# Seam of merge, routing and experts in a one-core encoder block: a wait moved, a tail reordered, small work moved between engines, and the last norm put into the experts stage

## The chip, the cores and the metric

The kernel runs on one core of one Trainium2 chip. The metric is the device time of one execution in microseconds (us), the median of several runs. A profiled execution has its own time, and inside it the span from its first instruction to its last.

## What is computed

One layer of a streaming encoder over 2048 tokens of 1024 features: two attention branches, a gated merge with an output projection, a mixture of experts (top group of 4, then the top 2 of its 8 experts), a last RMSNorm. Only the part from the merge's end on matters here:

```python
x = x + mixed @ w_out[l]
h2 = rmsnorm(x, norm_ffn[l])
x = x + hierarchical_moe(h2, ...)      # in it:
    g_logits = hf @ w_rg + b_rg                 # 4 groups
    e_logits = hf @ w_re + b_re                 # 32 experts
    g_sel = argmax(g_logits); top_v, top_i = top_k(e_logits of the group, 2)
    gate_w = p_group * softmax(top_v)
    # each expert's rows, in order of token, in tiles; for each tile
    a = silu(xb @ w_eg[e]) * (xb @ w_eu[e]);  y = a @ w_ed[e]
    out[row_tok] += y * row_w
return rmsnorm(x, norm_final)
```

All matrix products are float32 in three products of parts: each operand is split into a high part (rounded to fp32r) and the remaining low part (names `_hi`, `_lo`). ScalarE writes the high parts, VectorE and GpSimd the low ones.

## The kernel before

The program is a chain of stages (`project`, `attend`, `merge`, `route`, `experts`, `finish`). In a stage each engine has its own instruction list, in the order in which the code is written, and the engines meet only through semaphores. Between stages all engines meet: the block ends with a drain and a barrier (L60), then `Stage.__exit__` clears the stage's semaphores on GpSimd and runs another barrier (L63, L64). Three stages close together after the experts: `ex`, `weights` and `routes`; after `finish` one closes (`fn`).

**merge** goes over 8 blocks of 256 tokens, each with two tiles t of 128. TensorE runs block 0 apart and blocks 1 to 7 as one loop (`over_block`). At a block's end it multiplies the mixed rows with `w_out` (8 steps k of 6 products for each t, L1639). VectorE adds x (L1565), takes part in the RMS statistics and writes the normed row h (L1569); ScalarE squares, takes the root and stores x2 and h2. The router's logits of a tile need h turned by TensorE (`turn_h`, L1593), copied to SBUF as hT by ScalarE (`copy_h`, L1437), multiplied with the router's weights (`route_h`, L1600) and biased on VectorE (`logits`, L1532). For blocks 0 to 6 this happens inside the next block; for the last one it stands at the very end, tile 0 and then tile 1.

**route** works on all 2048 tokens at once, mostly as one chain on VectorE in which each operation waits for the one before (`then`). Constants are set first (13 memsets on VectorE, L1818 to L1821). Group and experts are picked with one-hot tensors laid out [token tile t, expert e]. Two products count rows: `upper` x `both` gives the rank within a tile, `ones` x `both` the sum of each tile. VectorE adds up the 16 tiles' sums one after another (`base`, L1869), adds the rank (L1870), and from slot numbers builds one-hot tensors: `tile_is` (L1892), `row_hot` (L1895), `tile_hot` parts 0 and 1 (L1898, L1900). Part 2, the low part of the weights, is on GpSimd (L1773). TensorE gathers them in 32 products (L1798), which are read out at L1907 to L1912. SyncE meanwhile loads expert 0's weights.

**experts** goes over 32 experts, each with at least one tile of 128 rows, with the weights of the next expert split while the current one is computed. TensorE's `step` for tile n is: gate product, turn of the previous tile's a, up product, turn of the next tile's x (`turn_x`), and the down product of the previous tile; in the very first step that down product has a zero `a` behind it. For expert 0 the wait for its down weights' low parts (`d_lo_pool`, `d_lo_dve`) stands ahead of the whole step. GpSimd gathers rows of h2 and adds result rows to x2 by indirect DMA (L2012); its last act is to wait until these are in DRAM.

**finish** loads x2 again, 16 tiles of 128 rows of 4 KB, through 8 input buffers by SyncE's queue, and g_row (`norm_final` on all partitions); ScalarE squares, takes roots, VectorE does the rest (`mean_square`, `inverse_rms`, L2319), GpSimd's queue stores the 16 tiles from 4 buffers (L2289).

## Time and profile before

| what | value |
|---|---|
| median of 3 runs | 2535.26 us (2533.03 to 2535.77) |
| the profiled execution | 2534.02 us |
| its span | 2532.3 us |
| TensorE busy in the span | 2304.2 us, 91% |
| VectorE, ScalarE, GpSimd busy | 51%, 40%, 34% |
| merge's last product ends to the first expert product | about 1570 to 1657 us of the span |
| last row added by the experts to the end | about 2476 to 2532 us |

The profile lists for each engine what ran when, what it did between (idle, with the inferred releaser), the granted TensorE clock (1.00 is 2.4 GHz, 0.50 is 1.2 GHz), and the DMA engines' share. TensorE is nearly always busy inside a stage; the idle stretches lie at the seams.

### The profile page before, as it was taken

Reading aid. Unit: us, or ns where it says so; the run is one execution under the profiler, and the core shown is the slowest. Engines: PE = TensorE matmul, PEld = TensorE weight load, DVE = VectorE, ACT = ScalarE, POOL = GpSimd, SP = SyncE. Lnnn points to the kernel's source line nnn. Section 1 sums busy time; section 2 is a strip of 40 time slices with the busy share of each in tenths; the row PEclk is TensorE's granted clock in tenths of the full one; section 3 lists DMA queues with packets and bytes.
Section 4 is the critical chain, followed back from the end, with each engine's and each line's share of the span. In section 5 each row is a group of like instructions: output and inputs, shape, how many; then the busy total and the mean of one; then the engine's idle time right before and its main releaser. Section 6 shows DMA issues by size and latency. Waiting matters only on the chain. (4 is left out here: it accounts for less than half of the span.)

```text
span 2532.3 us, 36785 instructions
## 1 busy us (share of the span) xinstructions
PE 2304.2 (91%) x12238; PEld 1976.1 (78%) x12239; DVE 1303.3 (51%) x1953; ACT 1023.1 (40%) x1778; POOL 854.8 (34%) x796
## 2 busy tenths in 40 slices
PE   7999999999996889986999998289999999999990
PEld 5888888888885788885999998268888888888870
DVE  5112223111002777775433333767857768788874
ACT  6111112111113777773222211146646556667653
POOL 5354665520000111112223221134444535455451
PEclk9999999999998999998999999589999999999995
DMA  5357757531115676636544442479978979899977
GB/s 179 106 148 263 251 173 240 177 115 61 73 58 200 172 229 170 196 83 205 179 140 141 141 141 91 144 240 307 321 227 272 327 226 323 281 370 346 317 254 282
DMA packets 234881, 517.34 MB, mean 204 GB/s; under 512 B 24368, under 2 KB 90032, under 8 KB 233648
## 3 DMA queue, kind: packets, MB, share of 16 engines
q1 hardware_dynamic: 159104, 342.28, 39.1%
q0 software_dynamic: 32352, 95.18, 15.0%
q10 hardware_dynamic: 43344, 78.86, 8.7%
q8 instruction: 44, 0.72, 0.1%
q14 instruction: 37, 0.30, 0.0%
HBM read 384.56 MB, written 131.66 MB: 204 GB/s over the span
## 5 line engine op out<-in xcount | busy, mean ns | idle before, releaser
L440 DVE TENSOR_TENSOR pj_w_lo<-pj_w_raw,pj_w_hi 128x1024 fp32r<-128x1024 f32 x38 | 48.0, 1263 | 520.0 <-ACT pj_w_hi L314 520.0
L314 ACT ACTIVATE pj_w_hi<-pj_w_raw 128x1024 fp32r<-128x1024 f32 x38 | 40.2, 1059 | 529.9 <-PE pj_bank L538 477.7
L2024 POOL TENSOR_TENSOR ex_wd_lo<-weights_raw_d,ex_wd_hi 128x1024 fp32r<-128x1024 f32 x64 | 199.4, 3138 | 124.1 <-ACT ex_wd_hi L2052 124.1
L538 PE MATMUL pj_bank<-pj_hT_hi,pj_w_lo 128*128 128x512 f32 x896 | 239.5, 389 | 0.0
L538 PE MATMUL pj_bank<-pj_hT_hi,pj_w_hi 128*128 128x512 f32 x896 | 239.5, 389 | 0.0
L538 PE MATMUL pj_bank<-pj_hT_lo,pj_w_hi 128*128 128x512 f32 x896 | 239.5, 389 | 0.0
L538 PEld LDWEIGHTS pj_bank<-pj_hT_lo,pj_w_hi 128*128 128x128 f32 x896 | 168.2, 188 | 34.9
L538 PEld LDWEIGHTS pj_bank<-pj_hT_hi,pj_w_hi 128*128 128x128 f32 x896 | 168.2, 188 | 34.9
L538 PEld LDWEIGHTS pj_bank<-pj_hT_hi,pj_w_lo 128*128 128x128 f32 x896 | 168.2, 188 | 34.8
L2106 DVE TENSOR_TENSOR ex_wd_lo<-weights_raw_d,ex_wd_hi 128x1024 fp32r<-128x1024 f32 x64 | 164.4, 2607 | 5.0 <-ACT ex_wd_hi L2052 4.9
L1615 PE MATMUL mg_y_ps<-mg_aT_hi,mg_w_hi 128*128 128x256 f32 x512 | 148.9, 291 | 9.8 <-DVE mg_gated L1526 6.6
L2172 PE MATMUL ex_g_ps<-ex_wg_hi,ex_xT_hi 128*128 128x512 f32 x360 | 141.0, 392 | 13.9 <-DVE ex_wd_lo L2106 13.9
L2100 DVE TENSOR_TENSOR ex_wu_lo<-weights_raw_u,ex_wu_hi 128x1024 fp32r<-128x1024 f32 x128 | 152.3, 1249 | 2.1
L2172 PE MATMUL ex_y_ps<-ex_wd_hi,ex_aT_hi 128*128 128x512 f32 x368 | 148.6, 404 | 1.9 <-DVE ex_aT_lo L2112 1.9
L2100 DVE TENSOR_TENSOR ex_wg_lo<-weights_raw_g,ex_wg_hi 128x1024 fp32r<-128x1024 f32 x128 | 147.8, 1214 | 3.6 <-ACT ex_wg_hi L2052 3.6
L854 POOL DMA_DIRECT2D scratch_attT<-at_o_both x60 | 49.7, 866 | 288.2 <-DMA scratch_attT<-at_o_both 288.2
L1390 POOL TENSOR_TENSOR mg_gated<-mg_gated 128x256 f32<-128x256 f32 x64 | 53.7, 840 | 274.0 <-DVE mg_gated L1526 273.5
L1616 PE MATMUL mg_y_ps<-mg_aT_lo,mg_w_hi 128*128 128x256 f32 x512 | 145.8, 285 | 0.0
L1617 PE MATMUL mg_y_ps<-mg_aT_hi,mg_w_lo 128*128 128x256 f32 x512 | 145.8, 285 | 0.0
L2172 PE MATMUL ex_u_ps<-ex_wu_hi,ex_xT_hi 128*128 128x512 f32 x360 | 144.9, 402 | 0.0
L2172 PE MATMUL ex_y_ps<-ex_wd_lo,ex_aT_hi 128*128 128x512 f32 x368 | 144.7, 393 | 0.0
L2172 PE MATMUL ex_y_ps<-ex_wd_hi,ex_aT_lo 128*128 128x512 f32 x368 | 143.7, 391 | 0.0
(289 smaller groups left out, 5920.1 us busy)
## 6 DMA issues: line engine op xcount, KB each, us to landing
weights_raw_g<-in_w_exp_gate_dram SPq DMA_DIRECT2D x128, 512.0 KB
weights_raw_u<-in_w_exp_up_dram SPq DMA_DIRECT2D x128, 512.0 KB
weights_raw_d<-in_w_exp_down_dram SPq DMA_DIRECT2D x128, 512.0 KB
pj_w_raw<-in_w_feat_dram SPq DMA_DIRECT2D x38, 512.0 KB, 4.8
scratch_gates<-pj_f_hi ACTq DMA_DIRECT2D x32, 512.0 KB, 5.0
mg_g_in<-scratch_gates SPq DMA_DIRECT2D x128, 128.0 KB, 3.1
pj_x_in<-in_x_dram SPq DMA_DIRECT2D x16, 512.0 KB, 3.6
scratch_qk<-pj_f_hi ACTq DMA_DIRECT2D x16, 512.0 KB, 5.1
```

The costliest lines, as they stand in the source:

```text
L314: act.activation(w_hi[n % 2][:], w_raw[n % 2][:], ACT.Copy).then_inc(whi_done, 1)
L440: dve.tensor_tensor(w_lo[n % 2][:], w_raw[n % 2][:], w_hi[n % 2][:], ALU.subtract).then_inc(wlo_done, 1)
L538: last = pe.matmul(eight[4 * p + b][:], w[p][:, k * P:(k + 1) * P], h[:, k, b * NB:(b + 1) * NB], start=(k == 0 and n == 0), stop=(k == KD ...
L854: pool.dma_start(attT[A_COLS + hd * DH:A_COLS + (hd + 1) * DH, at:at + WIDE], o_both[pair % 4][DH:, :], accum_op=ALU.add).then_inc(lo_out[ ...
L1390: pool.tensor_tensor(mixed[o % 2], gated[o % 2][:, :MB], gated[o % 2][:, MB:], ALU.add).then_inc(mixed_done, 1)
L1615: pe.matmul(y, w_hi[:, k, cols], aT_hi[:, k, :], start=(k % 4 == 0), stop=False)
L1616: pe.matmul(y, w_hi[:, k, cols], aT_lo[:, k, :], start=False, stop=False)
L1617: last = pe.matmul(y, w_lo[:, k, cols], aT_hi[:, k, :], start=False, stop=(k % 4 == 3))
L2024: pool.tensor_tensor(wd_lo[p][:, j, :], raw.buffer[2][j][:], wd_hi[p][:, j, :], ALU.subtract).then_inc(d_lo_pool, 1)
L2100: dve.tensor_tensor(slabs(lo, m, j), raw.buffer[m][j][:], slabs(hi, m, j), ALU.subtract).then_inc(lo_done, 1)
L2106: dve.tensor_tensor(wd_lo[p][:, j, :], raw.buffer[2][j][:], wd_hi[p][:, j, :], ALU.subtract).then_inc(d_lo_dve, 1)
L2172: last = pe.matmul(out, xT_parts[x][:, k, :], w_parts[w][:, k, cols], start=(k == 0 and c == 0), stop=(k == xT_parts[2] - 1 and c == 2))
```

## The change

1. **merge.** TensorE runs the last block apart from the loop (loop over blocks 1 to 6). In it the turn of tile 0's h stands inside the products of tile 1, ahead of k = 6 (`TURN_AT`); after the block: `route_h` of tile 0, `turn_h` of tile 1, `route_h` of tile 1. ScalarE copies hT of each tile right after that tile's h2 store.
2. **route.** The 12 priority memsets and `one_row` go to GpSimd, with three more for `ones` and a mask `going_on`; VectorE waits for them (`prio_set`, `zeroed`). The one-hot tensors are laid out [expert, token tile]. The sums over tiles come from one scan over 512 elements (`up_to`) and a subtraction (`ahead`) on VectorE; a second product, `ones` x `ahead`, is added in PSUM to the first, and a third of 32 columns gives the counts. The 16 adds, their memset and one more add are gone. The low parts are made by ScalarE in 32 operations of 64 columns, not by GpSimd. `row_hot` is written in halves, after `tile_hot`, and TensorE starts on a half.
3. **experts.** In the first step the wait for the down weights stands ahead of the down product, not ahead of the step.
4. **last norm.** It is part of the experts' stage. Buffers are the 12 raw weight buffers and x_in, y: one for g_row, 4 for output, 9 for input. g_row is loaded when its buffer comes free, the square root's table after the last `aT_hi`. When GpSimd's last rows are in DRAM it counts `all_added`, on which SyncE starts the loads. Stores are issued by SyncE too, each behind the load for the tile nine further on. ScalarE's order is root(t), square(t+1); VectorE's is the inverse of t, mean of t+1, product of t.

```diff
@@ merge @@
-            for t in range(2):
-                copy_h(NBLK - 1, t)
+                    if not more:
+                        copy_h(i, t)
...
+                        if end_of_all and t == 1 and k == TURN_AT:
+                            turn_h(i, 0)
...
-            with pe.Fori(1, NBLK) as i:
+            with pe.Fori(1, NBLK - 1) as i:
                 over_block(i, True)
-            for t in range(2):
-                turn_h(NBLK - 1, t)
-                route_h(NBLK - 1, t)
+            over_block(NBLK - 1, True, end_of_all=True)
+            route_h(NBLK - 1, 0)
+            turn_h(NBLK - 1, 1)
+            route_h(NBLK - 1, 1)
@@ route @@
+            for g in range(GROUPS):
+                pool.memset(prio4[:, :, g], float(GROUPS - g)).then_inc(prio_set, 1)
+            for e in range(PER_GROUP):
+                pool.memset(prio8[:, :, e], float(PER_GROUP - e)).then_inc(prio_set, 1)
             pool.memset(ones[:], 1.0).then_inc(zeroed, 1)
+            pool.memset(going_on[:, :, 1:], 1.0).then_inc(zeroed, 1)
+            pool.memset(going_on[:, :, :1], 0.0).then_inc(zeroed, 1)
+            pool.memset(one_row[:], 1.0).then_inc(zeroed, 1)
...
+            act.wait_ge(weight_split, 1)
+            for k in range(2):
+                act.wait_ge(tile_is_done, k + 1)
+                for t in range(NT):
+                    last = act.activation(tile_hot[k][:, t, 2, :], tile_is[k][:, t, :], ACT.Copy,
+                                          scale=weight_lo[k][:, t:t + 1].bitcast(F32))
+                last.then_inc(low_hot_done, 1)
...
+            pe.matmul(ranks, upper[:], both[:].rearrange("p e t -> p (e t)"), start=True, stop=False)
+            pe.wait_ge(count_asked, 2)
+            pe.matmul(ranks, ones[:], ahead[:].rearrange("p e t -> p (e t)"), start=False, stop=True)
+            pe.matmul(count_ps[:], ones[:], up_to[:, :, NT - 1], start=True, stop=True).then_inc(counted, 1)
...
+            then(dve.tensor_tensor_scan(up_to[:].rearrange("p e t -> p (e t)"), going_on[:].rearrange("p e t -> p (e t)"),
+                                        both[:].rearrange("p e t -> p (e t)"), 0.0, ALU.mult, ALU.add))
+            dve.tensor_tensor(ahead[:], up_to[:], both[:], ALU.subtract).then_inc(count_asked, 1)
...
-            for t in range(NT):
-                then(dve.tensor_tensor(base[:, t + 1, :], c_ps[1][:, t, :], base[:, t, :], ALU.add))
-            then(dve.tensor_tensor(rank[:], c_ps[0][:], base[:, :NT, :], ALU.add))
@@ experts @@
                 turn_x(n + 1)
+                if down_split:
+                    pe.wait_ge(d_lo_pool, 2)
+                    pe.wait_ge(d_lo_dve, 2)
                 down(n, p)
...
                 if first_of_all:
-                    pe.wait_ge(d_lo_pool, 2)
-                    pe.wait_ge(d_lo_dve, 2)
-                    step(first, p, e)
+                    step(first, p, e, down_split=True)
@@ last norm, SyncE @@
+            sp.wait_ge(all_added, 1)
...
+            for t in range(SUMS):
+                load_sum(t)
+            for t in range(NT):
+                sp.wait_ge(normed, t + 1)
+                if t + SUMS < NT:
+                    load_sum(t + SUMS)
+                sp.dma_start(out[t * P:(t + 1) * P, :], done[t % 4]).then_inc(stored[t % 4], 16)
```

TensorE's list at the end of merge, before (L1639 the last products, L1593 turns, L1600 router products):

```order
L1639 MATMUL mg_o_ps<-mg_w_hi,mg_mix_lo 128x512 x2
L1658 REGISTER_ALU
L1658 COMPARE_AND_BRANCH
L1593 MATMUL mg_o_ps<-mg_idt,mix_raw 128x128 [waits pj_ro_stored]
L1593 MATMUL mg_o_ps<-mg_idt,mix_raw 128x128 x7
L1600 MATMUL mg_o_ps<-mg_w_r,mg_hT 128x36 [waits at_sink_set]
L1600 MATMUL mg_o_ps<-mg_w_r,mg_hT 128x36 x7
L1593 MATMUL mg_o_ps<-mg_idt,mix_raw 128x128 [waits pj_ro_stored]
L1593 MATMUL mg_o_ps<-mg_idt,mix_raw 128x128 x7
L1600 MATMUL mg_o_ps<-mg_w_r,mg_hT 128x36 [waits at_sink_set]
L1600 MATMUL mg_o_ps<-mg_w_r,mg_hT 128x36 x7
L60 UNCONDITIONAL_BRANCH
```

and in the change (L1642, L1594 and L1601 are the same lines of code):

```order
L1594 MATMUL mg_o_ps<-mg_idt,mix_raw 128x128 [waits pj_ro_stored]
L1594 MATMUL mg_o_ps<-mg_idt,mix_raw 128x128 x7
...
L1642 MATMUL mg_o_ps<-mg_w_hi,mg_mix_hi 128x512 x2
L1642 MATMUL mg_o_ps<-mg_w_lo,mg_mix_hi 128x512 x2
L1642 MATMUL mg_o_ps<-mg_w_hi,mg_mix_lo 128x512 x2
L1601 MATMUL mg_o_ps<-mg_w_r,mg_hT 128x36 [waits at_sink_set]
L1601 MATMUL mg_o_ps<-mg_w_r,mg_hT 128x36 x7
L1594 MATMUL mg_o_ps<-mg_idt,mix_raw 128x128 [waits pj_ro_stored]
L1594 MATMUL mg_o_ps<-mg_idt,mix_raw 128x128 x7
L1601 MATMUL mg_o_ps<-mg_w_r,mg_hT 128x36 [waits at_sink_set]
L1601 MATMUL mg_o_ps<-mg_w_r,mg_hT 128x36 x7
L60 UNCONDITIONAL_BRANCH
```

The turn of tile 0 moved in front of the last two steps k (twelve products), and the router products of tile 0 in front of the turn of tile 1.

TensorE's list at the first expert, before (`ex_g_ps` gate product, L2187 turn of x, `ex_y_ps` down product; semaphores carry the names of their first users: `pj_wlo_done` and `pj_whi_done` are `d_lo_dve` and `d_lo_pool`):

```order
L1966 TENSOR_LOAD routes_first
L1966 ISA x2
L1967 TENSOR_LOAD routes_last
L1967 ISA x2
L2202 ISA [waits pj_wlo_done,pj_whi_done]
L2204 REGISTER_ALU [waits pj_hi_stored0]
L2172 MATMUL ex_g_ps<-ex_wg_hi,ex_xT_hi 128x512 [waits pj_w_ready1,pj_lo_stored1]
...
L2187 MATMUL ex_x_ps<-ex_idt,ex_x_in 128x128 [waits pj_plain_out]
L2187 MATMUL ex_x_ps<-ex_idt,ex_x_in 128x128 x7
L2172 MATMUL ex_y_ps<-ex_wd_hi,ex_aT_hi 128x512 [waits at_aq_in0,at_ak_in2]
```

and in the change:

```order
L2000 TENSOR_LOAD routes_first
L2000 ISA x2
L2001 TENSOR_LOAD routes_last
L2001 ISA x2
L2287 ISA
L2289 REGISTER_ALU [waits pj_hi_stored0]
L2257 MATMUL ex_g_ps<-ex_wg_hi,ex_xT_hi 128x512 [waits pj_w_ready1,pj_lo_stored1]
...
L2272 MATMUL ex_x_ps<-ex_idt,ex_x_in 128x128 [waits pj_plain_out]
L2272 MATMUL ex_x_ps<-ex_idt,ex_x_in 128x128 x7
L2257 MATMUL ex_y_ps<-ex_wd_hi,ex_aT_hi 128x512 [waits at_ak_in2,at_aq_in0,pj_wlo_done,pj_whi_done]
```

Both waits moved from ahead of the gate product to the first down product.

SyncE's list at the end, before (from the loop over the experts' weights on):

```order
L1984 REGISTER_ALU
L1984 COMPARE_AND_BRANCH
L60 UNCONDITIONAL_BRANCH
L2270 UNCONDITIONAL_BRANCH [waits barrier_Pool_Activation_PE_DVE_SP_release]
L2273 DMA fn_x_in<-scratch_x 128x1024 x2
L2277 DMA fn_g_row<-in_norm_final_dram 128x1024
L2273 DMA fn_x_in<-scratch_x 128x1024 x6
L2273 DMA fn_x_in<-scratch_x 128x1024 [waits pj_h_done] x8
L60 UNCONDITIONAL_BRANCH
```

and in the change (the input tiles lie in the old weight buffers, x_in and y):

```order
L2018 REGISTER_ALU
L2018 COMPARE_AND_BRANCH
L2030 DMA weights_raw_g<-in_norm_final_dram 128x1024 [waits pj_w_ready1]
L2037 DMA weights_raw_u<-scratch_x 128x1024 [waits pj_wlo_done,at_padded,pj_whi_done,pj_w_scaled]
L2037 DMA weights_raw_u<-scratch_x 128x1024 x2
L2037 DMA weights_raw_d<-scratch_x 128x1024 x4
L2037 DMA ex_x_in<-scratch_x 128x1024
L2037 DMA ex_y<-scratch_x 128x1024
L2037 DMA weights_raw_u<-scratch_x 128x1024 [waits ex_normed]
L2045 DMA out_dram<-weights_raw_g 128x1024
L2037 DMA weights_raw_u<-scratch_x 128x1024 [waits ex_normed]
L2045 DMA out_dram<-weights_raw_g 128x1024
```

The loads stand behind a wait in the same stage, and each store behind a load.

## Rows read from the trace of the kernel before

**Rows 1.** Windows, experts stage: us, busy PE, PEld, DVE, ACT, POOL, clock, DMA.
```profile
1710.00:1728.00 18.00, 18.00 (x87) 14.96 (x86) 18.00 (x16) 15.09 (x18) 11.54 (x6) 1.00 0.95 327
...
sum 828.00, PE 808.03 PEld 670.45 DVE 621.38 ACT 479.60 POOL 382.37; mean PE 17.57 PEld 14.57 DVE 13.51 ACT 10.43 POOL 8.31
```

**Rows 2.** Timeline, TensorE: start, us, line, tiles, [idle before <- releaser].
```profile
1569.67 1.03 PE L1593 MATMUL mg_o_ps<-mg_idt,mix_raw 128*128 128x128 f32 x8
...
1583.14 3.63 PE L1600 MATMUL mg_o_ps<-mg_w_r,mg_hT 128*128 128x36 f32 x16 [1.17 <-ACT mg_hT L1437]
1599.42 2.05 PE L1790 MATMUL rt_c_ps<-rt_both,rt_upper 128*128 128x512 f32 x2 [12.64 <-DVE rt_both L1854]
...
1640.84 1.94 PE L2187 MATMUL ex_x_ps<-ex_idt,ex_x_in 128*128 128x128 f32 x8 [8.41 <-DMA ex_x_in<-scratch_h,ex_rows]
1656.64 0.77 PE L2172 MATMUL ex_g_ps<-ex_wg_hi,ex_xT_hi 128*128 128x512 f32 x1 [13.85 <-DVE ex_wd_lo L2106]
...
1670.88 0.47 PE L2172 MATMUL ex_y_ps<-ex_wd_hi,ex_aT_hi 128*128 128x512 f32 x1
```

**Rows 3.** Timeline, VectorE, merge tail to first expert.
```profile
1573.70 1.28 DVE L1569 SCALAR_TENSOR_TENSOR mix_raw<-mix_raw,mg_stat,mg_g_row 128x1024 f32<-128x1024 f32 x1
...
1588.06 0.53 DVE L1818 MEMSET rt_prio<- 128x16 f32 x4 [1.05 <-PEq L64]
1588.67 1.14 DVE L1820 MEMSET rt_prio<- 128x16 f32 x8
...
1592.16 1.06 DVE L1840 TENSOR_REDUCE rt_inner<-rt_wide 128x128 f32<-128x512 f32 x1
...
1603.36 3.56 DVE L1869 TENSOR_TENSOR rt_base<-rt_c_ps,rt_base 128x32 f32<-128x32 f32 x16
...
1608.33 0.22 DVE L1875 TENSOR_TENSOR_SCAN rt_ends<-rt_one_row,rt_tiles_f 128x32 f32<-128x32 f32 x1
...
1610.88 0.69 DVE L1885 TENSOR_REDUCE rt_slot_f<-rt_picked 128x16 f32<-128x512 f32 x1
...
1613.92 2.36 DVE L1892 TENSOR_TENSOR rt_tile_is<-rt_place_row,rt_tile_f 128x1024 f32<-128x1024 f32 x2
...
1620.11 2.92 DVE L1898 TENSOR_TENSOR rt_tile_hot<-rt_tile_is,rt_ids 128x1024 fp32r<-128x1024 f32 x1
...
1626.29 1.21 DVE L1898 TENSOR_TENSOR rt_tile_hot<-rt_tile_is,rt_ids 128x1024 fp32r<-128x1024 f32 x1
...
1632.55 0.22 DVE L1907 TENSOR_SCALAR routes_token<-rt_token_ps 128x64 uint32<-128x64 f32 x1 [3.23 <-PE rt_token_ps L1798]
...
1643.45 1.29 DVE L2124 TENSOR_TENSOR ex_xT_lo<-ex_x_ps,ex_xT_hi 128x512 fp32r<-128x512 f32 x2 [2.13 <-ACT ex_xT_hi L2065]
...
1650.55 5.53 DVE L2106 TENSOR_TENSOR ex_wd_lo<-weights_raw_d,ex_wd_hi 128x1024 fp32r<-128x1024 f32 x2 [1.04 <-ACT ex_wd_hi L2052]
```

**Rows 4.** Windows of 1 us, columns as in Rows 1, after merge's last products.
```profile
1575.00:1576.00 1.00, 0.00 (x0) 0.00 (x0) 0.00 (x0) 0.55 (x2) 0.00 (x0) 0.78 0.15 61
```

**Rows 5.** Timeline, ScalarE's exponential and GpSimd's low parts, routing.
```profile
1590.52 0.26 ACT L1780 ACTIVATE rt_g_exp<-rt_g 128x64 f32<-128x64 f32 x1 [1.26 <-DVE rt_g L1835]
...
1615.30 6.65 POOL L1773 TENSOR_TENSOR rt_tile_hot<-rt_tile_is,rt_weight_lo 128x1024 fp32r<-128x1024 f32 x2 [27.12 <-DVE rt_tile_is L1892]
```

**Rows 6.** GpSimd's drains, line 60 (ns min/median/max, starts), and the chain of waits.
```profile
L60 POOLq DRAIN  x1: 4546/4546/4546, 2475.9 to 2475.9; - x1
...
2482.13 0.34 SPq L2273
...
L60 POOLq DRAIN  x1: 1356/1356/1356, 2530.2 to 2530.2; - x1
```

**Rows 7.** Windows, last norm, columns as in Rows 1.
```profile
2486.00:2490.00 4.00, 0.00 (x0) 0.00 (x0) 0.49 (x4) 3.53 (x6) 0.00 (x0) 0.50 1.00 346
...
2500.00:2505.00 5.00, 0.00 (x0) 0.00 (x0) 3.93 (x13) 2.48 (x6) 1.06 (x2) 0.50 1.03 420
```

**Rows 8.** DMA issues of route: KB each, median us from issue to landing.
```profile
rt_upper<-in_strict_upper_dram SPq DMA_DIRECT2D x1, 64.0 KB, 1.8
```

More of the change, by code:

```diff
@@ L1668 @@
 CHUNKS = 4
+ROW_PARTS = 2
 class Raw:
@@ L1701, in route @@
         logit = routes.logit
-        c_ps = [st.ps(f"c_ps{b}", [P, NT, EXPERTS]) for b in range(2)]
+        rank_ps = st.ps("rank_ps", [P, EXPERTS, NT])
+        count_ps = st.ps("count_ps", [P, EXPERTS])
         token_ps = st.ps("token_ps", [P, 3, MAX_TILES])
@@ L1815, in over @@
                 return ap.unsqueeze(2).broadcast_to([P, NT, m])
-            for g in range(GROUPS):
-                then(dve.memset(prio4[:, :, g], float(GROUPS - g)))
-            for e in range(PER_GROUP):
-                then(dve.memset(prio8[:, :, e], float(PER_GROUP - e)))
-            then(dve.memset(one_row[:], 1.0))
             g_logit = logit[:, :, :GROUPS]
@@ L2164, in _ @@
             y_out(end)
+            dve.wait_ge(const_in, 16)
+            dve.wait_ge(all_added, 1)
+            mean_square(dve, stat[0], 0, ssq_done, mean_done)
+            for t in range(NT):
+                inverse_rms(dve, stat[t % 4], t, root_done, rstd_done)
+                if t + 1 < NT:
+                    mean_square(dve, stat[(t + 1) % 4], t + 1, ssq_done, mean_done)
+                if t >= 4:
+                    dve.wait_ge(stored[t % 4], 16 * (t // 4))
+                dve.scalar_tensor_tensor(done[t % 4], sums_in[t % SUMS], stat[t % 4][:, 4:5], g_row,
+                                         ALU.mult, ALU.mult).then_inc(normed, 1)
         @block.tensor
```

157 lines of the change are left out of this document (68 added, 89 removed).

## The prediction

> **What bounds the kernel now.** I read the windows of the experts stage first, then the idle gaps of TensorE with their releasers, then VectorE's timeline inside those gaps. Inside the experts stage TensorE is never idle: 46 windows of 18 us have 808.0 us of 828 busy, and the 20 missing lie in the first window and the last two [rows 1]. So the experts cost what TensorE costs, and whatever starts their first product earlier ends them earlier by as much. The change touches none of that work. It touches what lies between the merge's last product, ended by about 1569.7 us, and the first gate product at 1656.64 [rows 2]: 87 us in which TensorE has some 20 us of work and VectorE's chain sets the pace. And it touches the last 56 us, where stage ends, DMA and VectorE take turns.
>
> **Merge's tail.** Before, tile 1's normed row is ready at 1573.70 + 1.28 = 1574.98 [rows 3], but tile 0's router products come first, and tile 1's own end at 1583.14 + 3.63 = 1586.77 [rows 2]. In the change tile 0's turn stands inside tile 1's products and delays them, and with them tile 1's row, by the 1.03 us of eight turns at most [rows 2]: about 1575.9. Tile 0's copy and products are over before that. Then a turn, a copy, the products. TensorE's clock: it reads 1.00 on average until the middle of the 1575 to 1576 window, whose mean is 0.78 (1.00 is 2.4 GHz, 0.50 is 1.2 GHz), after about 5 us without work [rows 4]. In the change tile 0's router products follow the last product (1569.7 + 0.9 for the turn inside + 1.8 at the full clock = 1572.4), and TensorE is without work for about 3.5 us, to 1575.9, so I take the lower clock, with turns at 1.94 and the router products at 3.63 as in the rows, and 1.17 for the copy [rows 2]: 1575.9 + 1.9 + 1.2 + 3.6 = 1582.6, against 1586.8. **Gain 4.2 us**; with the clock kept the turn is 1.03 and the products half of 3.63, gain 6.9; with nothing else late the low end is 3.5. The h2 store of tile 1 lies beside this.
>
> **Routing, constants.** Twelve of VectorE's memsets run from 1588.06 to 1588.67 + 1.14 = 1589.81, and a thirteenth small one behind [rows 3]: 1.9 us at the head of the chain. GpSimd, which does nothing else there, has four small ones (0.13 each by VectorE's row) to make before VectorE asks for them, in about the time of VectorE's first operations; it makes the other twelve while the chain goes on. Gain 1.8.
>
> **Routing, ranks.** Before, from the end of `both` (TensorE starts 0.15 us later, at 1599.42) to the first of the 16 adds at 1603.36 it is 4.1 us, two products of about 1.85 us each one after the other [rows 2, 3]. The adds take 3.56, the memset ahead of them 0.1 and the 512-element add behind them 0.7 (a pass over 512 elements is 0.69) [rows 3]: 8.4 us in all. After: scan, then subtraction 0.7, while the first product runs; then the second product 1.85, the 32-column one 0.45 (two passes at 3.63 / 16), 0.15 to wake VectorE. The scan is the unknown. Bounds: 0.69 as any pass of 512 elements, and 1.4 at twice that; the 32-element scan takes 0.22 [rows 3], so a scan is no cheap operation and I take 1.3. At 1.3 the first product (2.0) and the scan with the subtraction (2.0) end together: 2.0 + 0.1 + 1.85 + 0.45 + 0.15 = 4.6. Gain 8.4 - 4.6 = 3.8, the same down to a scan of 0.7. The new layout makes four VectorE operations write or read at a stride (two `hot`, two sums). The one strided reduce before takes 1.06 where the contiguous one takes 0.69 [rows 3]; that may be its 128 outputs. From 0 to 0.37 each, I take 0.4 for the four. Net 3.4.
>
> **Routing, one-hots.** GpSimd's low parts take 6.65 us from 1615.30 on [rows 5], and beside them VectorE's `tile_hot` takes 2.92, without them 1.21 [rows 3]. Before, from the start of `tile_is` at 1613.92 to the read-out at 1632.55: 18.6 us. After, with 1.15 for each 1024 elements (1.21 with overlap) and 2.36 for `tile_is`: k = 0 `tile_hot` done at 4.7, halves of `row_hot` at 5.8 and 6.95; k = 1: 9.25, then 10.4 and 11.55. TensorE needs about 0.23 a product, as for the router's (3.63 / 16 [rows 2]), 1.84 a half: from 6.95 to 8.8 at the latest for k = 0, then from 10.4 to 12.3 and on to 14.1; read-out at 14.5. Gain 4.1. This has ScalarE as cover: 32 operations of 64 columns. The nearest row is an exponential of 64 columns, 0.26 [rows 5]: 16 are 4.2 us, so k = 0 is ready at 5.4 (needed at 5.9) and k = 1 at 9.6 (needed at 10.5). At 0.20 they have more room; at 0.35 k = 1 comes at 12.4 and costs 2. **Routing in all: 1.8 + 3.4 + 4.1 = 9.3 us**, 7 to 11.
>
> **First expert.** The first gate product at 1656.64 is released by `wd_lo`, which ends at 1650.55 + 5.53 = 1656.08; its other input, `xT_lo`, is there at 1643.45 + 1.29 = 1644.74 [rows 2, 3]. So the gate product moves to about 1644.85: **gain 11.8 us**. Where does the wait go? From gate to down product it is 1670.88 - 1656.64 = 14.2 us [rows 2], so the down product is reached at 1659.1, 3.0 us after `wd_lo` (same clock of the stage). The wait costs nothing there. Behind it VectorE is late against TensorE by 2.1 us more than before, since `wd_lo` still ends at 1656.1 and only then comes `aT_lo` (0.7 us, wanted at 1659.1) and the next expert's split. In some windows VectorE is busy 18.00 of 18 [rows 1]; but before the first such stretch it has waits of some us for TensorE, in which this is taken back. SyncE's loads hang on VectorE's splits, so they shift with VectorE, not with TensorE. From 11 to 12.6 (the clock may rise a little later or sooner under the gate product).
>
> **The last norm.** Before: GpSimd's waits for the last rows end as its drain starts, at 2475.9; the drain takes 4.55 us, three stage ends follow, and the first load is issued at 2482.13 [rows 6]: 2482.13 - 2480.45 = 1.7 us for the three, 0.56 each. After, SyncE is released at 2475.9 in the same stage and the drain runs beside: loads start 6.2 us earlier. In the middle DMA is the bound: the share is 1.03 at 420 GB/s [rows 7], and 16 loads and 16 stores of 0.52 MB remain. g_row (0.52 MB, 1.25 us at 420 GB/s) is out of it. Against that the stores share a queue with the loads: the first store stands behind ten loads, 5.2 MB or 15 us at 346 GB/s [rows 7], so it lands some 17 us after the first load was issued, and only then may VectorE write its fifth tile. Between a gain of 1.25 and a loss of one or two I give the middle a gain of 0.5. At the end GpSimd's drain of 1.36 us [rows 6] is gone, since GpSimd has drained long ago, but three stage ends stand there instead of one, 2 x 0.56 more: 0.3. **Gain 7.0 us**, 3 to 10.
>
> **Sum.** 4.2 + 9.3 + 11.8 + 7.0 = 32.3 us. The span 2532.3 becomes 2500.0 and the profiled execution 2534.0 becomes 2501.7. The median of the runs is 1.2 above the profiled execution: 2535.3 - 32.3 = 2503.0.
>
> **Rivals.**
> *One queue for the last norm is slower than two.* If loads and stores in one queue move at the 346 GB/s of loads alone and not at the 420 of both kinds [rows 7], the 16 loads and first 7 stores (12.1 MB) take 35 us and not 29, some 2 less for VectorE's slack: 4 to 5 us lost, result about 2507.5. For it: the share is 1.00 at 346. Against: stores alternate with loads after the tenth. The Trainium skill (DMA: Bandwidth & Descriptors, Queues, rings and completion order) has each DMA engine alternate between the queues that have work and consume one queue in order. By that rule the stores lose the turn that a queue of their own gave them; the share of 1.03 shows full engines but not whose turn it was.
> *More than counted:* the clock stays at 2.4 GHz over tile 1's turn and products (2.7 us), the scan and strides cost little (1), the norm gains from its ninth buffer (2 to 3): about 2497.
> *ScalarE's low parts come late,* 0.35 each: 2505.
> *Slower than before: TensorE's code is fetched again.* The unrolled block pushes the experts' loop to another place in its code. If its 15 passes had to fetch code again, twice a pass, each fetch for no less than the 1.8 us in which a transfer of 64 KB lands in routing [rows 8], that is 15 x 2 x 1.8 = 54 us against the gain of 32.3: 2535.3 - 32.3 + 54 = 2557. It decides from 32.3 / 15 = 2.2 us a pass. Against: TensorE shows no idle in these passes now [rows 1], with a loop body of the same length. The Trainium skill (Runtime: NRT & Kernel Launch, Instruction fetch mechanics) says that a taken branch to code outside the fetched window waits for a fetch by DMA; no row here shows such a wait.
>
> **How the numbers follow.** The forecast as summed, 2498 to 2506.5: 0.62. The queue rival, to 2511: 0.19 (low parts late, within the same span, included). More gain, 2494 to 2498: 0.12. A partial gain eaten by something unseen at a seam, 2511 to 2530: 0.03. Within 0.2% (5 us, about what a measurement can tell from no change): 0.01. Slower: 0.03. The range 2494 to 2511 holds the first three, 0.93 by these chances, and takes in the bounds of all four terms but for the norm's low end together with other losses. Faster 0.96, same 0.01, slower 0.03.
>
> **What would show each step.** Merge: tile 1's router products right behind its turn, ending about 13 us after the last product. Routing: the stage from its first memset to its read-outs some 9 us shorter, the scan at 1.2 to 1.4, `tile_hot` at 1.2 without a neighbour, no wait of TensorE for ScalarE. Experts: gate product released by `xT_lo`, no gap ahead of the first down product, windows of 18 us full throughout. Norm: first load issued less than 0.3 us after the last rows land; the store-queue rival by the fifth product's wait for its buffer. The prediction is wrong if ScalarE's 16 operations exceed 5 us, if TensorE has a gap in the loop, or if the middle of the norm is longer than 45 us.

## The result, and where the 33 us came from

| | before | changed |
|---|---|---|
| median of the runs | 2535.5 us (4 runs) | 2500.8 us (4 runs) |
| profiled execution's span | 2532.3 us | 2499.6 us |

The ratio is 0.9869, 95% interval 0.9855 to 0.9883. The forecast was 2503.0 in a range of 2494 to 2511.

A sum that comes out right can hide terms that are wrong. So I split both spans at the same nine events: the start of the span, seven starts of operations that both kernels have, and the end. Each cell is the time from the event named to the next one; the last column is what the prediction said.

| stretch | before | changed | gained | forecast |
|---|---|---|---|---|
| start to merge's first `w_out` product | 1197.2 | 1199.9 | -2.7 | 0 |
| to route's first VectorE operation | 390.9 | 386.8 | 4.1 | 4.2 |
| to the first read-out of the one-hot products | 44.5 | 35.3 | 9.2 | 9.3 |
| to the first gate product | 24.1 | 12.5 | 11.6 | 11.8 |
| to the first down product | 14.2 | 13.8 | 0.4 | 0 |
| to the issue of the last added rows | 798.5 | 796.3 | 2.2 | 0 |
| to the first load of the last norm | 12.8 | 6.6 | 6.1 | 6.2 |
| to the end | 50.2 | 48.4 | 1.7 | 0.8 |
| sum | 2532.3 | 2499.6 | 32.7 | 32.3 |

Four terms stand almost as forecast. Two stretches that no edit touches (the start, and the long one of the experts) moved by 2 to 3 us each, in opposite directions; what they are, a run of the unaltered kernel tells (below).

TensorE, timeline of the changed kernel (start, us, line, tiles, in brackets the idle time ahead and its releaser), to be held against [rows 2]:

```profile
1569.67 1.03 PE L1594 MATMUL mg_o_ps<-mg_idt,mix_raw 128*128 128x128 f32 x8
...
1573.28 1.87 PE L1601 MATMUL mg_o_ps<-mg_w_r,mg_hT 128*128 128x36 f32 x16
...
1578.65 1.97 PE L1594 MATMUL mg_o_ps<-mg_idt,mix_raw 128*128 128x128 f32 x8 [3.50 <-DVE mix_raw L1570]
1581.80 3.63 PE L1601 MATMUL mg_o_ps<-mg_w_r,mg_hT 128*128 128x36 f32 x16 [1.18 <-ACT mg_hT L1438]
...
1630.23 1.94 PE L2272 MATMUL ex_x_ps<-ex_idt,ex_x_in 128*128 128x128 f32 x8 [8.42 <-DMA ex_x_in<-scratch_h,ex_rows]
1634.37 0.76 PE L2257 MATMUL ex_g_ps<-ex_wg_hi,ex_xT_hi 128*128 128x512 f32 x1 [2.20 <-DVE ex_xT_lo L2195]
```

and VectorE's part of `wd_lo` in the same kernel:

```profile
1639.95 5.67 DVE L2177 TENSOR_TENSOR ex_wd_lo<-weights_raw_d,ex_wd_hi 128x1024 fp32r<-128x1024 f32 x2 [1.05 <-ACT ex_wd_hi L2107]
```

At merge's end only tile 1's turn and products are left behind its row, both at the lower clock (1.97 and 3.63), after an idle stretch of 3.50 us, as the prediction had it. The gate product is released by `xT_lo`, 2.20 us behind the turn of x, where it waited 13.85 us for `wd_lo`. No row with a wait stands ahead of the first down product: it starts at 1648.17, 2.55 us after `wd_lo` ends at 1645.62 (3.0 in the prediction).

Route, timelines of VectorE and ScalarE, against [rows 3, 5]:

```profile
1593.79 2.06 DVE L1868 TENSOR_TENSOR rt_hot<-rt_g_hot,rt_hot 128x512 f32<-128x512 f32 x2
1595.88 0.69 DVE L1871 TENSOR_TENSOR rt_both<-rt_hot 128x512 f32<-128x512 f32 x1
...
1596.72 1.23 DVE L1874 TENSOR_TENSOR_SCAN rt_up_to<-rt_going_on,rt_both 128x512 f32<-128x512 f32 x1
...
1600.76 0.19 DVE L1889 TENSOR_SCALAR rt_cnt_i<-rt_count_ps 128x32 int32<-128x32 f32 x1 [0.18 <-PE rt_count_ps L1812]
...
1603.98 1.00 DVE L1902 TENSOR_REDUCE rt_slot_f<-rt_picked 128x16 f32<-128x512 f32 x1
...
1607.66 2.36 DVE L1909 TENSOR_TENSOR rt_tile_is<-rt_place_row,rt_tile_f 128x1024 f32<-128x1024 f32 x2
1608.98 7.75 ACT L1799 ACTIVATE rt_tile_hot<-rt_tile_is,rt_weight_lo 128x64 fp32r<-128x64 f32 x32 [15.03 <-DVE rt_tile_is L1909]
1609.94 1.22 DVE L1913 TENSOR_TENSOR rt_tile_hot<-rt_tile_is,rt_ids 128x1024 fp32r<-128x1024 f32 x1
...
1621.92 0.23 DVE L1928 TENSOR_SCALAR routes_token<-rt_token_ps 128x64 uint32<-128x64 f32 x1 [2.14 <-PE rt_token_ps L1819]
```

The scan of 512 elements takes 1.23 us, the strided sum 1.00 where the contiguous one took 0.69, ScalarE's low parts 7.75 / 32 = 0.24 each, and `tile_hot` 1.22, without a neighbour.

The last norm: GpSimd's drain, the load, VectorE's fifth product and the middle (columns of the window as in [rows 1]):

```profile
L60 POOLq DRAIN  x1: 4546/4546/4546, 2451.1 to 2451.1; - x1
```

```profile
2451.12 1.29 SPq L2037 DMA_DIRECT2D weights_raw_u<-scratch_x  x3
```

```profile
2468.12 1.28 DVE L2248 SCALAR_TENSOR_TENSOR weights_raw_g<-weights_raw_d,ex_stat,weights_raw_g 128x1024 f32<-128x1024 f32 x1 [1.80 <-DMA out_dram<-weights_raw_g]
```

```profile
2471.00:2476.00 5.00, 0.00 (x0) 0.00 (x0) 4.09 (x13) 2.50 (x7) 0.00 (x0) 0.50 1.03 421
```

The drain of 4.55 us begins as the first load is issued, and nobody waits for it. The middle runs at 421 GB/s and a share of 1.03, as with two queues [rows 7]. The fifth product, the prediction's sign for its queue rival, waits 1.80 us for the store that frees its buffer; before the change it was 0.44:

```profile
2499.28 1.28 DVE L2319 SCALAR_TENSOR_TENSOR fn_done<-fn_x_in,fn_stat,fn_g_row 128x1024 f32<-128x1024 f32 x1 [0.44 <-DMA out_dram<-fn_done]
```

### The profile page after: what moved, and what is told of

It reads as the page before. It is cut to its first block and busy times, and to the rows that moved or that the text cites. A ratio compares the mean times of both kernels' runs of the same rounds, so it can differ in the third digit from the quotient of the medians.

```text
span 2499.6 us, 36776 instructions
## 1 busy us (share of the span) xinstructions
PE 2301.8 (92%) x12240; PEld 1976.8 (79%) x12241; DVE 1300.0 (52%) x1927; ACT 1031.5 (41%) x1811; POOL 845.1 (34%) x793
```

## The experiments

All times below are held against 2500.8 us of the changed kernel, or 2535 of the one before (2534.0 to 2535.4 where it ran beside the experiments). Since single executions scatter by 2 to 3 us, I read the terms from the same events as above. In the diffs, `...` stands for lines left out.

### The wait for the down weights

```diff
-                if down_split:
-                    pe.wait_ge(d_lo_pool, 2)
-                    pe.wait_ge(d_lo_dve, 2)
...
                 if first_of_all:
-                    step(first, p, e, down_split=True)
+                    pe.wait_ge(d_lo_pool, 2)
+                    pe.wait_ge(d_lo_dve, 2)
+                    step(first, p, e)
```

> The changed kernel with one part undone: TensorE's wait for the down weights' low parts stands ahead of the first step again. My theory (the whole wait was idle time and nothing behind it is late): the first gate product comes 11.4 to 11.8 us later, the experts end as much later, time 2500.8 + 11.6 = 2512.4 us. The rival (the wait comes back behind the first step, since VectorE is then later against TensorE): VectorE takes back part of it within the first two experts, so undoing costs less than 9 us, below 2510, and the changed kernel shows an idle gap ahead of the first or second down product that this one has not.

Measured 2514.6 us, ratio to the kernel before 0.9918 (0.9895 to 0.9941). From the read-out to the gate product 24.2 us against 12.5: 11.7, all of the term. The other 2 us lie elsewhere: merge began 1.1 later, and gate to down took 14.7 against 13.8, since TensorE's products came at the full clock only 5.3 us after the gate product and not 3.4 (see below, what belongs to one execution). The wait came back nowhere: theory upheld.

### Merge's tail: which of the two reorderings works

```diff
-                        if end_of_all and t == 1 and k == TURN_AT:
-                            turn_h(i, 0)
...
-            route_h(NBLK - 1, 0)
-            turn_h(NBLK - 1, 1)
-            route_h(NBLK - 1, 1)
+            for t in range(2):
+                turn_h(NBLK - 1, t)
+                route_h(NBLK - 1, t)
```

> The changed kernel with merge's tail as before: tile 0's turn and router products and then tile 1's, behind the last product; the last block still stands apart from the loop, and the copies stand where the change puts them. My theory (the gain is tile 0's turn, copy and products taken off tile 1's path, less the turn put inside): from the last w_out product to route's first VectorE operation 4.8 us longer, 0.8 of it given back by the turn, so 4.0 slower: 2504.8 us. The rival, the measured 1.4 us by which route began earlier is the whole gain: 2502.2. If this kernel begins merge's first w_out product at the time of the kernel before, the late start lies in the execution and not in the unrolled block.

Measured 2501.7 us. My expectation of 4.0 us was wrong. From the first `w_out` product to route it is 386.3 us, which is 0.45 *less* than in the changed kernel (386.8; the six other traces with the same merge have 386.65 to 386.81). TensorE's order, the part of this edit that the prediction spoke of, gains nothing. What this kernel still has of the change is ScalarE's place for the copies. Two kernels tell the two apart: the one before with the copies alone moved, and the changed one with the copies alone moved back.

```diff
 (kernel before)
                     act.dma_start(h2[ds(i * MB + t * P, P), :], h_t[t][:]).then_inc(h_out[t], 16)
+                    if not more:
+                        copy_h(i, t)
...
-            for t in range(2):
-                copy_h(NBLK - 1, t)
```

> The kernel before with one edit: in merge's last block ScalarE copies hT of a tile right behind that tile's h2 store, not both at the end. The new theory of merge's tail (what held it was tile 0's copy, which stood behind tile 1's square and store on ScalarE; the place of the turn on TensorE gives nothing): from the last w_out product to route's first VectorE operation 14.3 us in place of 18.9, so 4.6 faster: 2535.4 - 4.6 = 2530.8 us. The old theory of the prediction (the order on TensorE holds it): less than 1 us of gain, 2534.5 or above.

> The changed kernel with ScalarE's two copies of hT at the very end again, TensorE's order as changed. New theory: tile 0's copy then waits for tile 1's normed row and tile 0's router products stand behind it, ahead of tile 1's turn: from the last w_out product to route's first operation 18 us or more in place of 13.8, 4 to 5 us slower, 2505.3 us. Old theory: TensorE's order keeps most of the gain, at most 1.5 us slower, 2502.3.

The first measured 2529.2 us (ratio 0.9979, 0.9969 to 0.9988, ten runs), 386.4 us for the stretch: all of the gain. The second measured 2507.2 us and 391.7 for the stretch: all of it lost, and 0.8 more than before the change, which leaves TensorE's new order as the cause (that the last block stands apart costs nothing: 386.3 with it and 386.4 without, both with early copies and the old order). ScalarE and TensorE in the kernel before:

```profile
1575.45 1.08 ACT L1437 ACTIVATE mg_hT<-mg_o_ps 128x512 f32<-128x512 f32 x2 [2.63 <-DVE mix_raw L1569]
1576.59 3.63 PE L1600 MATMUL mg_o_ps<-mg_w_r,mg_hT 128*128 128x36 f32 x16 [5.89 <-ACT mg_hT L1437]
```

in the changed kernel with late copies:

```profile
1577.44 1.06 ACT L1475 ACTIVATE mix_raw<-mix_raw 128x1024 f32<-128x1024 f32 x1 [10.20 <-DVE mix_raw L1566]
...
1581.64 1.09 ACT L1438 ACTIVATE mg_hT<-mg_o_ps 128x512 f32<-128x512 f32 x2 [2.62 <-DVE mix_raw L1570]
1582.77 3.62 PE L1601 MATMUL mg_o_ps<-mg_w_r,mg_hT 128*128 128x36 f32 x16 [6.76 <-ACT mg_hT L1438]
1586.20 1.95 PE L1594 MATMUL mg_o_ps<-mg_idt,mix_raw 128*128 128x128 f32 x8
```

and in the kernel before with early ones:

```profile
1570.56 1.03 PE L1593 MATMUL mg_o_ps<-mg_idt,mix_raw 128*128 128x128 f32 x8
1571.64 1.08 ACT L1437 ACTIVATE mg_hT<-mg_o_ps 128x512 f32<-128x512 f32 x2 [8.79 <-PE mg_o_ps L1593]
1572.77 2.34 PE L1600 MATMUL mg_o_ps<-mg_w_r,mg_hT 128*128 128x36 f32 x16 [1.17 <-ACT mg_hT L1437]
1576.39 1.97 PE L1593 MATMUL mg_o_ps<-mg_idt,mix_raw 128*128 128x128 f32 x8 [1.28 <-DVE mix_raw L1569]
```

In the changed kernel with late copies, h of tile 0 was turned by 1573.3, but its copy stands in ScalarE's list behind tile 1's square, root and h2 store, and that store waits for tile 1's row. So tile 0's products (3.62 us at the lower clock) begin only when tile 1 is ready too. In the kernel before with early ones the copy follows the turn at once, and tile 0's products are over before tile 1's row is there.

### Route: constants, ranks, low parts

```diff
+            for g in range(GROUPS):
+                then(dve.memset(prio4[:, :, g], float(GROUPS - g)))
...
-                pool.memset(prio4[:, :, g], float(GROUPS - g)).then_inc(prio_set, 1)
```

> The changed kernel with 13 memsets of the priorities and one_row on VectorE again, ahead of its chain. Theory (they are at the head of the chain and nothing covers them): route's chain 1.9 us longer, 2502.7 us. Rival: VectorE waits there for GpSimd's constants in the changed kernel about as long, so under 0.5 us.

Measured 2504.8 us. Route's stretch is 37.6 us against 35.3, 2.4 longer; 1.95 of it is the memsets' time, from 1586.69 to the first operation at 1588.64, and 0.4 the second rank product and the count product, which ran wholly at TensorE's lower clock here and in part at the full one in the changed kernel. The rest of the 4.0 us between the medians is not route's (see below).

```diff
-            then(dve.tensor_tensor_scan(up_to[:]..., going_on[:]..., both[:]..., 0.0, ALU.mult, ALU.add))
-            dve.tensor_tensor(ahead[:], up_to[:], both[:], ALU.subtract).then_inc(count_asked, 1)
+            for t in range(NT):
+                then(dve.tensor_tensor(base[:, t + 1, :], count_ps[:, :, t], base[:, t, :], ALU.add))
+            then(dve.tensor_tensor(rank[:], rank_ps[:], base[:, :NT, :].rearrange("p t e -> p e t"), ALU.add))
```

> The changed kernel with the ranks as before: no scan, no subtraction, a product of ones with both and 16 adds of 32 elements one after another, in the new layout. My theory (3.8 us in the trace's terms: 8.4 for waiting, adds and the rank's add against 4.6): route's chain 3.5 to 4.5 us longer, 2504.8 us. A rival: the adds now read and write at a stride and cost more than the 0.22 us of before, 5 us or more. Another: part of the chain was hidden anyway behind TensorE's products, below 2 us.

Measured 2507.5 us, route's stretch 39.7: 4.5 longer, at the top of what I gave; the time is 2.7 above the expected one. The 16 adds take 3.57 us as before, the rank's add now 1.02, with one operand read at a stride.

```diff
+            pool.wait_ge(weight_split, 1)
+            for k in range(2):
+                pool.wait_ge(tile_is_done, k + 1)
+                pool.tensor_tensor(tile_hot[k][:, :, 2, :], tile_is[k][:], weight_lo[k][:]..., ALU.mult).then_inc(low_hot_done, 1)
...
-            act.wait_ge(weight_split, 1)
-            for k in range(2):
-                act.wait_ge(tile_is_done, k + 1)
-                for t in range(NT):
-                    last = act.activation(tile_hot[k][:, t, 2, :], ...)
-                last.then_inc(low_hot_done, 1)
```

> The changed kernel with the low parts of the weights made by GpSimd again, two operations of 1024 elements, all else as changed. Theory of contention between VectorE and GpSimd: GpSimd takes 3.3 us an operation, VectorE's operations beside it 1.7 us longer each as before (2.9 against 1.2), two or three of them: route's chain 3 to 5 us longer, 2504 to 2506. Rival, without contention: the first low part is ready at 3.3 us and the second at 6.6 us after tile_is, both ahead of need, so nothing is lost: 2500.8.

Measured 2505.6 us, route's stretch 39.1: 3.8 longer. VectorE and GpSimd there:

```profile
1607.09 2.92 DVE L1911 TENSOR_TENSOR rt_tile_hot<-rt_tile_is,rt_ids 128x1024 fp32r<-128x1024 f32 x1
1609.94 2.92 DVE L1913 TENSOR_TENSOR rt_tile_hot<-rt_tile_is,rt_weight_hi 128x1024 fp32r<-128x1024 f32 x1
1612.78 2.35 DVE L1917 TENSOR_TENSOR rt_row_hot<-rt_place_row,rt_row_f 128x1024 fp32r<-128x1024 f32 x2
...
1615.05 1.21 DVE L1911 TENSOR_TENSOR rt_tile_hot<-rt_tile_is,rt_ids 128x1024 fp32r<-128x1024 f32 x1
```

```profile
1606.19 5.58 POOL L1791 TENSOR_TENSOR rt_tile_hot<-rt_tile_is,rt_weight_lo 128x1024 fp32r<-128x1024 f32 x2 [21.49 <-DVE rt_tile_is L1907]
```

GpSimd's results are in time (both by 1611.8; the first half of `row_hot` ends at 1614). What is lost are 2 x 1.7 us on VectorE, whose two operations beside GpSimd's each take 2.92; the other 0.4 is the count product at the lower clock, as above. The 2.92 is a wait and then the operation: GpSimd's two end at 1608.93 and 1611.77, VectorE's at 1610.01 and 1612.85, each 1.08 later. In the kernel before, half of `row_hot`, twice as many elements, ended 2.15 after GpSimd's first one:

```profile
1616.20 3.99 DVE L1895 TENSOR_TENSOR rt_row_hot<-rt_place_row,rt_row_f 128x2048 fp32r<-128x2048 f32 x1
```

The Trainium skill (SBUF — State Buffer, SBUF: two separate sides) says that the two engines share a pair of ports, which an operation with two inputs in SBUF and one of GpSimd that reads SBUF hold as an exclusive lock for a whole instruction; these rows agree.

### The last norm: one queue or two

```diff
-                sp.dma_start(out[t * P:(t + 1) * P, :], done[t % 4]).then_inc(stored[t % 4], 16)
...
             pool.sem_inc(all_added, 1)
+            for t in range(NT):
+                pool.wait_ge(normed, t + 1)
+                pool.dma_start(out[t * P:(t + 1) * P, :], done[t % 4]).then_inc(stored[t % 4], 16)
...
```

> The changed kernel with the 16 stores of the last norm issued by GpSimd's queue, as before the change, and the loads by SyncE; all in the experts' stage. The rival of my forecast (one queue for loads and stores is slower): with a queue of their own the stores go beside the loads, the fifth output tile waits less, 3 to 5 us faster, 2496 to 2498. My theory (the 16 DMA engines are the bound either way, a store waits no longer behind loads than for the engines): within 1 us of 2500.8 in the middle, and GpSimd's drain, long past in the change, stands behind its stores again and costs 1 to 4 us: 2502 to 2505.

Measured 2505.9 us. From the first load to the start of the last product it is 41.6 us against 42.4: a queue of its own for the stores is worth 0.8 us, not 3 to 5 (the eleven traces with one queue have 42.2 to 43.3 there, so 0.6 to 1.7). The fifth product waits 1.19 for its buffer instead of 1.80. From there to the end it is 12.5 us against 6.1, since GpSimd's drain stands behind its stores again, and is longer than in the kernel before (1.36 [rows 6]):

```profile
L60 POOLq DRAIN  x1: 5852/5852/5852, 2497.4 to 2497.4; - x1
```

So in this shape of the block the stores' place on SyncE is worth some 5 us, nearly all of it through the drain. What the Trainium skill (DMA: Bandwidth & Descriptors, Queues, rings and completion order) says, that each engine alternates between the queues that have work, bears on the 0.8 alone.

### What belongs to one execution

> The changed kernel once more, unaltered, to separate what belongs to the kernel from what belongs to one execution. Two things differ between traces without a reason in the code: TensorE's step of one expert takes 17.69 or 17.73 us (44 steps, 1.8 us in all), and merge's first w_out product starts between 1196.8 and 1202.5 us. If they belong to the execution: the step may be 17.73 here, the start anywhere in that range, times from 2498 to 2504 us. If the step belongs to the kernel: 17.69 again, and the median within 1 us of 2500.8.

Measured 2500.9 us; the trace has 17.73 us a step where the first one had 17.69 (turn of x in two neighbouring steps, the first trace and the repeated kernel):

```profile
2072.02 1.03 PE L2272 MATMUL ex_x_ps<-ex_idt,ex_x_in 128*128 128x128 f32 x8
2089.71 1.03 PE L2272 MATMUL ex_x_ps<-ex_idt,ex_x_in 128*128 128x128 f32 x8
```

```profile
2070.93 1.03 PE L2272 MATMUL ex_x_ps<-ex_idt,ex_x_in 128*128 128x128 f32 x8
2088.66 1.03 PE L2272 MATMUL ex_x_ps<-ex_idt,ex_x_in 128*128 128x128 f32 x8
```

Merge began at 1197.9 us. So both belong to the execution: of 14 traces, 6 had 17.69 and the others 17.73, with no order by kernel, and merge's start lay between 1196.8 and 1202.5. Why a step has two lengths stays open; I found no wait in it. Of the 2.2 us that the stretch from the first down product was shorter, 0.04 x 44 = 1.8 are this; the last 0.4 is what is left of two others at its end (the last down product, partly at the lower clock, took 7.4 us before and 5.7 after, and VectorE then waited 1.2 us longer for an earlier store of result rows). The 2.7 that merge began later are the other. None of this is a property of the change.

A third such thing is when TensorE's clock rises under the first gate product. The first product at the full clock starts 4.3 us after it in the kernel before, 3.4 and 3.1 in the two executions of the changed one, and 5.2 to 5.7 in the runs with the wait, the low parts, the constants or the adds put back. What runs at 1.2 GHz takes twice as long, so gate to down takes 14.2, 13.8 and 13.75, and 14.7 to 14.9. It explains the 0.4 in the table, and 0.9 to 1.1 us of what these four runs are slower beyond their own stretch. Whether their later start sets it or chance does, these runs don't tell. Two windows, 4 us behind the gate product, the changed kernel and the one with GpSimd's low parts:

```profile
1638.00:1640.00 2.00, 2.00 (x10) 1.63 (x9) 0.95 (x2) 2.00 (x4) 1.90 (x1) 1.00 0.96 299
```

```profile
1638.50:1640.50 2.00, 2.00 (x6) 1.61 (x5) 0.97 (x1) 2.00 (x4) 1.83 (x1) 0.50 0.95 302
```

### Keeping TensorE's clock

At the seams TensorE comes back several times from a pause at 0.50 (1.2 GHz). Would work that nobody reads keep it at 1.00 (2.4 GHz)?

```diff
             route_h(NBLK - 1, 0)
+            for _ in range(14):
+                pe.matmul(y_ps[0][:]..., mix_hi[:, 0, :P], w_hi[:, KD, :NB], start=True, stop=True)
             turn_h(NBLK - 1, 1)
```

> The changed kernel with 14 products more (128x512, their result is never read) on TensorE between tile 0's router products and tile 1's turn at merge's end, where it was idle 3.5 us and its granted clock fell from 1.00 to 0.50. Theory that the clock follows what TensorE did just before: it stays at 1.00 over tile 1's turn (1.03 in place of 1.97) and router products (1.87 in place of 3.63), 2.7 us faster, 2498.1 us. Rival: the clock falls all the same at that place, nothing gained, and where the added products run past tile 1's row, up to 0.5 lost: 2501.3.

Measured 2497.0 us (ratio 0.9852, 0.9835 to 0.9868), and the stretch is 384.2 us against 386.8, 2.5 less; the other 1.3 between the medians I can't assign. Timeline and a window of it (the last three numbers of a window are clock, DMA share, GB/s):

```profile
1574.33 3.47 PE L1666 MATMUL mg_y_ps<-mg_w_hi,mg_mix_hi 128*128 128x512 f32 x14
1578.01 1.09 PE L1594 MATMUL mg_o_ps<-mg_idt,mix_raw 128*128 128x128 f32 x8 [0.21 <-DVE mix_raw L1570]
1580.27 1.98 PE L1601 MATMUL mg_o_ps<-mg_w_r,mg_hT 128*128 128x36 f32 x16 [1.17 <-ACT mg_hT L1438]
```

```profile
1580.00:1582.00 2.00, 1.73 (x16) 1.73 (x16) 0.00 (x0) 0.22 (x1) 0.00 (x0) 1.00 0.05 18
```

Then the same in all pauses up to the experts, each added group where the pause stood:

> The kernel with 14 added products at merge's end and further added products of 128 columns, never read, in every wait of TensorE in routing and at the experts' start (26 ahead of the rank product, 52 ahead of the one-hot products, 6 behind them, 14 ahead of the first turn of x, 7 behind it). Theory (the clock follows TensorE's work, and each of its pieces there is on the path): the second rank product and the counts 1.0 faster, the last half of the one-hot products 0.9, the turn of x 1.0, the first expert's gate to down 1.0 to 1.7, some 0.4 lost where an added product is in the way: 3.5 to 4.2 us below the kernel with the 14 alone (2497.0), 2493.2 us. Rival: between route and experts TensorE has no work for over 4 us whatever is added, so the clock falls there, and only route's part is gained: 1.5 us, 2495.5.

Measured 2498.2 us, not faster. In the trace route's first operation to the first down product is 59.5 us against 61.9 with the 14 alone, so 2.4 of the 4 us are there. But six added products behind the one-hot products and 14 ahead of the turn of x ran mostly at 0.50 and stood in the way (14 took 5.02 us; the row counts two passes for each); the read-out to the turn of x took 9.9 us against 8.1. And VectorE is now late for the first time:

```profile
1622.70 5.02 PE L2323 MATMUL ex_g_ps<-ex_idt 128*128 128x128 f32 x28 [2.57 <-DMA ex_idt<-in_ident_dram]
...
1649.20 0.47 PE L2267 MATMUL ex_g_ps<-ex_wg_hi,ex_xT_hi 128*128 128x512 f32 x1 [0.39 <-DVE ex_xT_lo L2205]
```

So what the experts' start gained was mostly given back at once. From the first down product to the second it is 19.08 us here and 17.7 in the kernels without these products, 1.4 more. With that, and with a step of 17.73 us here and 17.69 in the trace of the 14 alone, nothing is left of the 2.4.

A last version keeps 7 and 6 at the experts' start, 28, 57, 7 and 3 in route, and has the turn of tile 0 back behind the last product:

> A version made of what the runs showed: tile 0's turn behind the last product (not inside), with 4 added products (128x512) behind it and 7 behind tile 0's router products; in routing 28, 57, 7 and 3 added products of 128 columns in TensorE's waits; at the experts' start 7 ahead of the turn of x and 6 behind it. None of the added results is read. Against the kernel with 14 added products at merge's end (2497.0 us): 0.4 to 0.8 from the turn, 1.5 from route, 2.0 from the experts' start, as its predecessor with more of them showed between route's first operation and the first down product (59.5 against 61.9 us), and 0.5 from what its 6 and 14 badly placed ones cost. Theory: 2494.0 us. Rival: the clock falls between route and experts whatever is added, and the added products run there at the lower clock in the way of the turn: 2496.5.

Measured 2495.3 us, ratio 0.9843 (0.9827 to 0.9859), 5.5 below the changed kernel; against the version with 14 products the medians differ by 1.7 and the intervals overlap. Its trace has 58.7 us from route's first operation to the down product, 2.8 less than the changed kernel, and 384.2 for merge's stretch. The rival held at the experts' start, in a window over the turn of x:

```profile
1618.00:1628.00 10.00, 8.12 (x36) 7.73 (x37) 7.60 (x9) 6.20 (x8) 2.27 (x3) 0.50 0.74 250
```

Between route and experts TensorE has no work for 3.73 us, since the identity is loaded there, and the clock is back at 1.00 only in the window from 1628. That the identity be loaded a stage earlier wasn't tried. These traces speak against much gain from it: here too gate to down is 1.5 us shorter than with the 14 alone, and from there to the second down product it is 1.1 longer (18.79), since TensorE waits for VectorE ahead of the second gate and the second down product:

```profile
1658.77 0.50 PE L2273 MATMUL ex_y_ps<-ex_wd_hi,ex_aT_hi 128*128 128x512 f32 x1 [0.46 <-DVE ex_aT_lo L2199]
```

What this version has over the one with the 14 is route's stretch, 33.7 us against 35.6.

## Why the prediction was right, point by point

**What bounds.** Right. From the first gate product on, one wait of TensorE shows, 1.87 us ahead of the last down product (1.86 before the change), and every us at the seams was a us of the whole.

**Merge's tail, 4.2.** The size was right (4.1), the cause was not. The step that failed is "tile 0's router products come first": they came first on TensorE, but were late because ScalarE's copy stood behind tile 1's square and store. I read the row with the 5.89 us of idle and its releaser, `mg_hT`, and did not ask what ScalarE did in between. The turn inside tile 1's products, in which I saw the means, costs 0.45 us (386.8 against 386.3). That the clock would be at its lower level over tile 1's turn was right, but by luck: the row it was read from has it fall some 5 us after the last product, and the pause forecast was 3.5. In the changed kernel it fell about 1 us after tile 0's router products had ended at 1575.15; nothing here shows why so soon:

```profile
1576.00:1577.00 1.00, 0.00 (x0) 0.00 (x0) 0.61 (x4) 0.22 (x2) 0.00 (x0) 0.59 0.00 0
```

**Constants, 1.8.** 1.95.

**Ranks, net 3.4.** From `both`'s end to the counts' first operation 1607.68 - 1599.27 = 8.4 before (rows below), 1600.76 - 1596.57 = 4.2 after: 4.2 gained for 3.8 forecast, the scan at 1.23 in the upper half of 0.69 to 1.4. The Trainium skill (DVE: opcode table, instruction layouts, handler registers and perf-mode slots; Datapath and trigger behaviour) has the scan at half throughput; 1.23 is 1.8 times 0.69, which nearly agrees. The strides were under-sized: `hot` 2.06 for 1.42 and two sums of 1.00 for 0.69 each make 1.3, where I took 0.4. Net 2.9.

```profile
1597.13 1.42 DVE L1851 TENSOR_TENSOR rt_hot<-rt_g_hot,rt_hot 128x512 f32<-128x512 f32 x2
1598.58 0.69 DVE L1854 TENSOR_TENSOR rt_both<-rt_hot 128x512 f32<-128x512 f32 x1
...
1607.68 0.18 DVE L1872 TENSOR_SCALAR rt_cnt_i<-rt_base 128x32 int32<-128x32 f32 x1
```

**One-hots, 4.1.** 1632.55 - 1613.92 = 18.6 before, 1621.92 - 1607.66 = 14.3 after: 4.4. The cover held: 16 operations of ScalarE take 3.9 us and TensorE waits for `row_hot`, never for them. With GpSimd's low parts back, 3.4 of the 4.4 are lost; the other 1.0 I put down to the order and the halves of `row_hot`, which no run took back by itself. 1.95 + 2.9 + 4.4 = 9.2, the 9.3 forecast: what the strides cost more (0.9) and what the ranks and one-hots gave more (0.7) nearly cancel, which is luck.

**First expert, 11.8.** 11.6, and the undone edit gives 11.7. VectorE's lateness cost nothing; the two versions that reach the first down product 2.4 and 2.8 us sooner show where it begins (the second gate product and the second down product wait for it, and the step between the first two down products grows by 1.4 and 1.1 us).

**Last norm, 7.0.** 6.1 + 1.7 = 7.8. The earlier loads are right to 0.1, read from the traces: no run puts the norm back into a stage of its own. Middle and end were 0.9 too low in this trace, but in the repeated one that stretch is 49.0, a gain of 1.1. In the middle, the first product came 6.8 us after the first load and not 8.4, and 0.7 of these 1.6 us were lost again, mostly at the fifth product.

**Rivals.** One queue for two: right in direction, 0.8 us in size for 4 to 5, by one trace. Late low parts: no. TensorE's code fetched again: no; the steps are 17.69 to 17.73 us in both kernels. More than counted: the clock did fall in merge, and keeping it is worth the 2.5 us that the rival gave (2.7).

**The sum.** 32.7 against 32.3, but with -2.7, 0.4 and 2.2 in it that belong to the execution. The stretches that hold the edits give 4.1 + 9.2 + 11.6 + 7.8 = 32.7; the other three, -2.7, 0.4 and 2.2, happen to cancel in this pair of traces, which is luck. The profiled execution took 2501.3 us for 2501.7 forecast; the median is 2.2 below its forecast because it lay 1.2 above the profiled execution before and lies 0.5 below it now.

## What to carry to other kernels

When an engine waits for a copy, look in the copying engine's own list for what stands ahead of it, before the waiting engine is reordered: moving two lines on ScalarE gave 4.5 us, the reordered TensorE list cost 0.45. A wait that stands ahead of a whole step belongs ahead of the one product that needs it, when nothing else in the step does; here 11.7 us. And where one trace stands against another, split both at common events: a term that no edit touches shows the size of the scatter, here 2 to 3 us in one pair and 5.7 over 14 traces. And an engine that is brought forward gains only until the next one is late: TensorE's first expert, made 1.2 to 1.5 us shorter, gave nearly all of it back one step later.
